# One decoder step on one core: cross attention of prompt and decode woven into one unrolled sequence

## The reference, cut to what matters

```python
def cross_attention(xn, mem_k, mem_v, w_xq, w_xo):
    q = (xn @ w_xq).reshape(B, T, 4, 256)
    s = jnp.einsum('bqhd,bkhd->bhqk', q, mem_k) * 256 ** -0.5
    p = jax.nn.softmax(s, axis=-1)
    o = jnp.einsum('bhqk,bkhd->bqhd', p, mem_v).reshape(B, T, 1024)
    return o @ w_xo
```

## Time and profile before

| what | us |
|---|---|
| median of 3 runs (2057.16 to 2065.2) | 2058.48 |
| the profiled execution, its own time | 2059.77 |
| its span in the trace | 2058.0 |
| PE busy in the span | 1851.6 (90%) |
| DVE, ACT, POOL busy | 956.0, 513.2, 107.2 |

### The profile page before, as it was taken

How to read it: one execution, slowest core, us unless ns; L and a number is a source line. 1 busy time by engine, 2 the same in 40 slices (tenths; PEclk the granted TensorE clock), 3 DMA queues, 4 the chain that set the end, 5 groups by cost and what they waited for, 6 DMA issues and landing times.

```text
span 2058.0 us, 32104 instructions
## 1 busy us (share of the span) xinstructions
PE 1851.6 (90%) x12971; PEld 1669.7 (81%) x12971; DVE 956.0 (46%) x1127; ACT 513.2 (25%) x847; POOL 107.2 (5%) x141
## 2 busy tenths in 40 slices
PE   6699998989988978898896969999999999999993
PEld 4599896656557977797745958999999999999992
DVE  2614777877764258423302256343324332333445
ACT  2411213666555111403331132111000110001122
POOL 0000001000220001001010010000000000000000
PEclk7899999999998989999997979999999999999995
DMA  6311115666784114111043112111111211121003
GB/s 163 110 59 61 61 61 162 201 176 193 244 307 173 61 52 133 60 61 62 0 164 123 41 41 105 41 49 53 41 41 47 55 41 41 45 57 36 33 26 156
DMA packets 136998, 187.18 MB, mean 91 GB/s; under 512 B 7752, under 2 KB 99082, under 8 KB 136390
## 3 DMA queue, kind: packets, MB, share of 16 engines
q1 hardware_dynamic: 122032, 120.74, 19.1%
q0 software_dynamic: 14192, 64.53, 8.9%
q10 hardware_dynamic: 686, 0.73, 0.1%
HBM read 165.65 MB, written 20.74 MB: 91 GB/s over the span
## 4 chain that ended last, share of the span: by engine, by line
PE 81%; DVE 6%; ACT 6%; DMA 3%; issue 3%; SPq 1%; DVEq 0%; POOLq 0%; ACTq 0%; POOL 0%
PE PS L1619 19%; PE PS L1620 19%; PE PS L1621 19%; PE PS L1609 7%; PE PS L1781 2%; PE PS L1803 2%; PE PS L1827 2%; DMA bias_rows<-BVEC 2%; PE PS L2106 2%; PE PS L2082 1%; PE PS L1696 1%; ACT KTS L681 1%; PE PS L2066 1%; PE PS L1634 1%; PE PS L1864 1%
## 5 line engine op out<-in xcount | busy, mean ns | idle before, releaser
L1619 PE MATMUL PS<-XH,WH 128*128 128x352 f32 x1992 | 643.1, 323 | 0.0
L1620 PE MATMUL PS<-XL,WH 128*128 128x352 f32 x1992 | 638.6, 321 | 0.0
L1621 PE MATMUL PS<-XH,WL 128*128 128x352 f32 x1992 | 638.3, 320 | 0.0
L1084 DVE CAST WH<-RAW 128x1024 fp32r<-128x1024 f32 x128 | 97.2, 760 | 719.9 <-PE PS L1621 695.0
L1620 PEld LDWEIGHTS PS<-XL,WH 128*128 128x128 f32 x1992 | 374.3, 188 | 0.0
L1619 PEld LDWEIGHTS PS<-XH,WH 128*128 128x128 f32 x1992 | 373.7, 188 | 0.0
L1621 PEld LDWEIGHTS PS<-XH,WL 128*128 128x128 f32 x1992 | 373.4, 187 | 0.0
L1086 DVE TENSOR_TENSOR WL<-RAW,WH 128x1024 fp32r<-128x1024 f32 x128 | 158.9, 1242 | 4.4
L1199 DVE SCALAR_TENSOR_TENSOR CY<-GP,DW,CY 128x1024 f32<-128x1024 f32 x124 | 158.5, 1278 | 1.0 <-DVE CY L1202 1.0
L1619 PE MATMUL PS<-HH,WH 128*128 128x352 f32 x462 | 149.0, 323 | 0.0
L1620 PE MATMUL PS<-HL,WH 128*128 128x352 f32 x462 | 148.1, 321 | 0.0
(11 more groups left out here) (322 smaller groups left out, 2321.8 us busy)
## 6 DMA issues: line engine op xcount, KB each, us to landing
PG<-in_cache_k SPq DMA_DIRECT2D x128, 256.0 KB, 3.0
PG<-in_cache_v SPq DMA_DIRECT2D x64, 256.0 KB, 4.1
PG<-in_cache_v POOLq DMA_DIRECT2D x64, 256.0 KB, 4.4
RAW<-in_w_gate SPq DMA_DIRECT2D x22, 512.0 KB, 3.9
RAW<-in_w_up SPq DMA_DIRECT2D x22, 512.0 KB, 5.1
RAW<-in_w_in SPq DMA_DIRECT2D x20, 512.0 KB, 4.6
h_spill<-H POOLq DMA_DIRECT2D x2, 4224.0 KB, 13.9
H<-h_spill POOLq DMA_DIRECT2D x2, 4224.0 KB, 13.7
```

The costliest lines, as they stand in the source:

```text
L1084: dve.tensor_copy(WH[v % 2][:, :, :], raw).then_inc(hi_done, 1)
L1619: pe.matmul(out, WH[u][:, k, :], xh[:, k, cols], start=(k == 0), stop=False)
L1620: pe.matmul(out, WH[u][:, k, :], xl[:, k, cols], start=False, stop=False)
L1621: mm = pe.matmul(out, WL[u][:, k, :], xh[:, k, cols], start=False, stop=(k == kt - 1))
```

## The change

- Prompt and decode run in one unrolled sequence of nine steps (q from 0 to 8). In steps 0 to 3, the keys of two decode sequences are turned and scored among the prompt's matmuls (`CROSS_K`); in step 4 comes the decode softmax; in steps 5, 6 and 7, the decode values of three, three and two sequences (`CROSS_V`).
- The turns of the keys have one PSUM bank in place of two. CKT has four buffers, one for each head, and the decode scores of a sequence are issued at once, with the head as the inner loop.
- The prompt's scores have one pair of banks in place of two, and read the queries straight from Y. Q2S and its copies are gone.
- CKV has four buffers. The first two lie in scratch space of the norm, and their loads are issued once the norm's sums are done, during the query projection; the next two as before, when the last `xq` tile is done.
- OX is copied and turned in step 8, ahead of the last block of prompt values.

The diff, cut; the removed lines are those of the kernel above. Left out too are the bodies of DVE functions that only change their place.

```diff
+        CKV = [at(f"CKV{i}", [P, 2, D], F32, (R2B + 16384, R2B + 24576, R1, R1 + 8192)[i]) for i in range(4)]
+        XP = [at(f"XP{i}", [P, NH, NMEM], F32, R1 + 16384 + 4096 * i) for i in range(2)]
+        XPT = [at(f"XPT{i}", [P, 8, P], F32, R1 + 24576 + 4096 * i) for i in range(2)]
+        CKT = [at(f"CKT{i}", [P, 2, NMEM], F32, R1 + 32768 + 2048 * i) for i in range(NH)]
+        XS = at("XS", [P, NMEM], F32, R1 + 40960)
+        OX = at("OX", [P, NMEM], F32, R1 + 41984)
+        YZ = at("YZ", [P, KT, DB * (TS + DS)], F32, R1 + 43008)
...
+        CROSS_K, CROSS_V = {q: (2 * q, 2 * q + 1) for q in range(4)}, {5: (0, 1, 2), 6: (3, 4, 5), 7: (6, 7)}
...
+            def memory_in(n):
+                pool.dma_start(CKV[n % 4][:, :, :], ck[n] if n < DB else cv[n - DB]).then_inc(ck_in[n % 4], 16)
+            pool.wait_ge(n_x["summed"], KT)
+            for n in range(2):
+                memory_in(n)
+            pool.wait_ge(tile_done, TILE0["xo"] + AHEAD)
+            for n in range(2, 4):
+                memory_in(n)
...
+            for n in range(4, 2 * DB):
+                if n - 4 < DB:
+                    pool.wait_ge(ck_turned, 4 * (n - 4) + 4)
                 else:
+                    pool.wait_ge(cv_used, n - 4 - DB + 1)
+                memory_in(n)
...
+            def memory_taken(b, h):
+                act.wait_ge(ck_turned, NH * b + h + 1)
+                if b:
+                    act.wait_ge(cs_done, b)
+                copy(CKT[h][:, :, :].rearrange("p a t -> p (a t)"), PS[:, 2, :]).then_inc(ck_taken, 1)
+            def cross_exp(q, h):
+                act.activation(XP[q % 2][:, h, :], PSF[:, NMEM * h:NMEM * (h + 1)], ACT.Exp,
+                               bias=XNM[q % 2][:, h:h + 1], scale=XSCALE, accum_out=XSUM[q % 2][:, h:h + 1])\
+                    .then_inc(x_p, 1)
+            for q in range(QT + 1):
+                b = CROSS_K.get(q)
+                if q:
+                    act.wait_ge(x_pt, q)
+                    if q >= 3:
+                        act.wait_ge(x_pv, q - 2)
+                    copy(XPT[(q - 1) % 2][:, :, :].rearrange("p (a k) t -> p a (k t)", a=2), PS[:, 4:6, :]).then_inc(x_ptok, 1)
+                if b:
+                    for h in range(NH):
+                        memory_taken(b[0], h)
+                if q < QT:
                     act.wait_ge(x_negmax, q + 1)
+                    if q >= 2:
+                        act.wait_ge(x_pt, q - 1)
                     for h in range(NH):
+                        cross_exp(q, h)
+                        if b:
+                            memory_taken(b[1], h)
+                if q == 4:
+                    act.wait_ge(xsm_v, 2)
+                    act.activation(XS[:, :], PS[:, 3, 0:NMEM], ACT.Exp, bias=XNMS, scale=XSCALE, accum_out=XSUMS)\
+                        .then_inc(xsm_a, 1)
...
+            for q in range(QT + 1):
+                if q < QT:
+                    cross_max(q)
+                if q == 4:
+                    decode_max_cross()
+                if q < QT:
+                    cross_weights(q)
+                if q == 4:
+                    decode_weights_cross()
+                if q == QT:
+                    dve.wait_ge(cv_used, DB)
+                    dve.tensor_copy(OX[:, :], PS[:, 3, 0:NMEM]).then_inc(xsm_v, 1)
+                    dve.wait_ge(xsm_p, 2)
+                    for a in range(2):
+                        dve.tensor_copy(Y[:, a:KT:2, TP:T], PS[:, 2, P * a:P * a + P].rearrange("p (h t) -> p h t", h=NH))\
+                            .then_inc(xsm_v, 1)
+                if q:
+                    cross_out(q - 1)
+                if q == 4:
+                    decode_turned_cross()
...
+            def cross_scores(q, h):
+                if h == 0:
+                    pe.wait_ge(x_p, NH * q)
+                for k in range(2):
+                    x = pe.matmul(PSF[:, NMEM * h:NMEM * h + NMEM], Y[:, 2 * h + k, P * q:P * q + P],
+                                  KMT[:, 2 * h + k, :], start=(k == 0), stop=(k == 1))
+                if h == NH - 1:
+                    x.then_inc(xs_done, 1)
+            def cross_turn(q):
                 pe.wait_ge(x_pn, q + 1)
                 pe.wait_ge(x_ptok, q)
                 for h in range(NH):
                     for k in range(2):
                         n = 2 * h + k
+                        x = turn(PS[:, 4 + n // 4, P * (n % 4):P * (n % 4) + P], XP[q % 2][:, h, P * k:P * k + P])
                 x.then_inc(x_pt, 1)
+            def cross_values(q, n):
+                if n == 0:
+                    pe.wait_ge(x_ptok, q + 1)
+                    pe.wait_ge(x_out, q)
+                for d in range(2 * n, 2 * n + 2):
                     for k in range(2):
                         x = pe.matmul(PS[:, 6 + d // 4, P * (d % 4):P * (d % 4) + P], VM[:, k, P * d:P * d + P],
+                                      XPT[q % 2][:, 2 * (d // 2) + k, :], start=(k == 0), stop=(k == 1))
+                if n == 3:
+                    x.then_inc(x_pv, 1)
+            def memory_turn(b, h):
+                if h == 0:
+                    pe.wait_ge(ck_in[b % 4], 16 * (b // 4) + 16)
+                pe.wait_ge(ck_taken, NH * b + h)
                 for d in range(2):
                     for a in range(2):
+                        c = 2 * h + d
+                        x = turn(PS[:, 2, NMEM * d + P * a:NMEM * d + P * a + P], CKV[b % 4][:, a, P * c:P * c + P])
+                x.then_inc(ck_turned, 1)
+            def memory_scores(b):
+                pe.wait_ge(ones_ok, 11)
+                pe.wait_ge(ck_taken, NH * b + NH)
+                for d in range(2):
+                    for h in range(NH):
+                        x = pe.matmul(PS[32 * h:32 * h + 32, 3, 0:NMEM], YZ[:, 2 * h + d, TS * b:TS * b + TS],
+                                      CKT[h][:, d, :], start=(b == 0 and d == 0), stop=(b == DB - 1 and d == 1))
+                x.then_inc(cs_done, 1)
...
+            def memory_values(b):
+                n = DB + b
+                pe.wait_ge(ck_in[n % 4], 16 * (n // 4) + 16)
+                if b == 0:
+                    pe.wait_ge(xsm_v, 6)
+                for a in range(2):
+                    for h in range(NH):
+                        x = pe.matmul(PS[32 * h:32 * h + 32, 3, 0:NMEM], PTZ[:, a, h, TS * b:TS * b + TS],
+                                      CKV[n % 4][:, a, NMEM * h:NMEM * h + NMEM],
                                       start=(b == 0 and a == 0), stop=(b == DB - 1 and a == 1))
                 x.then_inc(cv_used, 1)
+            pe.wait_ge(memkv_taken, 4)
+            pe.wait_ge(psum_free, TILE0["xo"] + AHEAD)
+            for q in range(QT + 1):
+                keys, vals = CROSS_K.get(q), CROSS_V.get(q, ())
+                if q:
+                    cross_turn(q - 1)
+                for h in range(NH):
+                    if keys:
+                        memory_turn(keys[0], h)
+                    if q < QT:
+                        cross_scores(q, h)
+                    if h == 0 and q - 1 in CROSS_K:
+                        memory_scores(CROSS_K[q - 1][1])
+                for b in vals:
+                    memory_values(b)
+                if q == QT:
+                    pe.wait_ge(xsm_v, 7)
+                    for a in range(2):
+                        x = turn(PS[:, 2, P * a:P * a + P], OX[:, P * a:P * a + P])
+                    x.then_inc(xsm_p, 1)
+                for n in range(4):
+                    if keys:
+                        memory_turn(keys[1], n)
+                    if n == 0 and keys:
+                        memory_scores(keys[0])
+                    if q:
+                        cross_values(q - 1, n)
+                if q == 4:
+                    pe.wait_ge(xsm_v, 4)
+                    for a in range(2):
+                        x = turn(PS[:, 2, P * a:P * a + P], XS[:, P * a:P * a + P])
+                    x.then_inc(xsm_p, 1)
```

More of the change, by code:

```diff
@@ L204, in hymba_step @@
         KMTOK = at("KMTOK", [P, 2, D], F32, R1 + 24576)
[L206 to L216 removed]
+        CKV = [at(f"CKV{i}", [P, 2, D], F32, (R2B + 16384, R2B + 24576, R1, R1 + 8192)[i]) for i in range(4)]
[5 more added lines that the diff above has]
+        YZ = at("YZ", [P, KT, DB * (TS + DS)], F32, R1 + 43008)
+        PTZ = at("PTZ", [P, 2, NH, DB * (TS + DS)], F32, R1 + 52224)
         HST = [at(f"HST{i}", [P, KT, P], F32, R1 + 4096 * i) for i in range(2)]
@@ L414, in hymba_step @@
         x_out = sem("x_out")
-        ck_in = [sem(f"ck_in{i}") for i in range(2)]
+        ck_in = [sem(f"ck_in{i}") for i in range(4)]
         ck_turned = sem("ck_turned")
@@ L1000, in _ @@
             late_norm(n_x, NM, "x_pre")
-            act.wait_ge(psum_free, TILE0["xo"] + AHEAD)
+            act.wait_ge(mem_v_out, 16)
             act.wait_ge(tile_done, TILE0["xo"] + AHEAD)
-            act.wait_ge(mem_v_out, 16)
-            def stage_query(q):
```

(37 more changed lines are left out.)

133 lines of the change are left out of this document (24 added, 109 removed).

## The result

| | before | changed |
|---|---|---|
| median, us (runs beside each other) | 2060.7 (4 runs) | 2010.1 (4 runs, 2006.3 to 2011.7) |
| profiled execution, span | 2059.77, 2058.0 | 2010.85, 2009.3 |
| stage: last query write to first matmul of `xo` | 943.92 to 1109.65: 165.7 | 942.69 to 1060.23: 117.5 |

The ratio is 0.9748 (95% interval 0.973 to 0.9767): 2.5% faster. The forecast was 2011.5, with 2004 to 2028. The stage is 48.2 us shorter and the span 48.7, so the gain is the stage's: it starts 1.2 us earlier, and what lies behind it takes 0.7 us longer.

What follows compares the result with a forecast made beforehand. PE's in-order list, its work and idle time, was taken to bound the stage. Steps summed to 116.3 us, 49.5 less; a second clock fall left 47.2 saved from 2059.77, 2012.6, median 2011.5, range 2004 to 2028.

Steps and rivals of the forecast that it cites:

- step 4: Last carried-over decode scores, a prompt block and the decode softmax: 11.1 us, with PE idle 1.8 before the XS turns.
- step 8: OX turns, last prompt values and output copies before `xo`: 9.8 us, of which 3.8 idle at the end.
- low rate: Rival: column groups take 1.96 us a sequence for scores and values, bound by weight issue; saved 32, 2026; chance 0.12.
- no overlap: Rival: decode scores still take 3.92 us a sequence in the new order; saved about 17, 2041; chance 0.05.
- second low spell: Second half of step 0: the granted clock falls once more amid short turns and waits, costing about 2.3 us.
- step 0: First key turns and prompt scores, with no values to put between: 8.2 and 7.3 us for its halves, 15.5 together.
- step 1: First of three like steps weaving key turns, prompt scores, decode scores and values: 15.9 us each, before any low spell.
- steps 5 to 7: Prompt blocks with three, three and two sequences of decode values at 1.0 us each: 32.1 us.
- first low spell: Start of step 0: PE spends 4.8 us at granted clock 0.50 after idling, losing 2.4 us.
- The rival in which steps 0 to 3 stay at half clock: Turns do not count as busy, so PE's work doubles there; saved about 25, 2033; chance 0.06.
- from the side of what goes: Cross-check for the whole stage: 63 us of work and waits removed, 14 of new idle time, difference 49.
- The slower case: Rival: the woven sequence never regains full clock, taking 208 us in place of 116; 43 slower, 2101; chance 0.03.

Runs made afterwards that it cites:

- the other edits: Changed kernel with three key turns ahead of the last query write and carried-over decode scores ahead of the first head's prompt scores: stage 111.0 us, median 2004.9.
- one head at a time: Changed kernel with each head's decode scores issued by themselves, other PE work between heads: stage 136.2 us, median 2030.5.
- the profiled run with early turns: Changed kernel with three key turns before the last query write and carried-over decode scores ahead of the first head's prompt scores: stage 111.0 us, median 2004.9.
- the one with the filler too: Changed kernel with early key turns, reordered decode scores and 32 useless matmuls between key turns of step 0's second half: stage 108.8 us, median 2004.1.

## Why the prediction was right

- **Column groups.** 1.0 us for 16 instructions was forecast from half of the low-clock 1.96; the trace has 1.00 for scores and 0.91 for values, at a granted clock of 1.00. Taking them apart again costs 18.7 us. The rivals "low rate" and "no overlap" fall. The Trainium skill ("TensorEngine Tiling (Array Packing)", Overview: Theoretical Speedup) gives up to 4 times for dimensions of 32 or less; here it is 3.9 times (3.92 to 1.0). Against 16 instructions at the plain 0.216 it is 3.5 times; the rest is what the lone head cost above that, 0.98 against 0.865.
- **Step by step.** Forecast and trace, with the second low spell added to step 1: step 0, 15.5 and 16.0; step 1, 18.2 and 17.4; steps 2 and 3, 15.9 and 15.6 each; step 4, 11.1 and 11.4; steps 5 to 7, 32.1 and 31.6; step 8, 9.8 and 9.9. Sum 118.6 and 117.5. Part of the closeness of step 0 is luck: PE starts 0.36 behind the query write, which was not counted, and the first low spell lasted longer, but a key turn with its head's scores takes 1.35 and not 1.445. The idle of 0.78 behind the first head is there to the digit, and so are the ones near 1.8 before XS and 3.8 before `xo`. The forecast 0.2 ahead of the second turn is not there; the last exponentials cost 0.38, not 0.28; the idle before the OX turns is 0.78, not 0.95; the values were 0.09 cheaper each.
- **The clock.** It fell twice, at the places named. The second spell was put at 2.3 us; filling the gaps gave back 2.0 in the changed kernel and 2.2 with the other edits. For the first, PE needed until about 948.8, 5.8 us after its start, where I took 4.8. The rival in which steps 0 to 3 stay at half clock falls: the clock was 1.00 from 976.12 to 1007.32, steps 2 and 3.
- **Loads.** No idle time of PE is put down to a load. That this hung on the four buffers, for steps 5 and 6, and not for the keys, was not in the forecast, which spoke of cover in general; the run with two buffers shows it.
- **Where the forecast was right in sum for partly compensating reasons.** The account "from the side of what goes" put 23 on the scores, 21 on the values and 19 on the rest. The runs give 14 to 19 for the groups, 10 to 14 for buffers and loads, depending on what stands beside them, and 20 for weaving, because weaving is also what takes loads and CKT copies out of PE's way and keeps the clock up under the values. The sum, 48, is the same; the split by cause needed the experiments.
- **Slips in the working that decided nothing.** The rival without overlap was priced at 30 us (17 saved in place of 47), where eight sequences at 3.92 in place of 1.0 make 23; one head at a time measured 18.7. The slower case was said to need some 110 us of low clock out of 116. By its own figures, all 116 at low clock add 92 us, so some 62 of them use up the 49.5 gained; those would last some 110, which is to be held against the 166 of the stage before. And the clock was said to fall in 826 to 828 "where PE made only turns": in the 6 us before that PE made only turns too, and the clock was 1.00 (last section).

## What to carry to other kernels

When an engine with an in-order list stalls in several small ways, walk the new order step by step with durations from the old trace, and for each wait ask what stands before it in every queue: here that gave the stage to 1 us in 118. The four-way split of the array paid here only with all four heads' operands there together, so it needed four copies of the operand's buffer, and then loads that keep up (17.6 us with four load buffers, 14.3 with two). And where a step must wait, put work there, real work first: real turns ahead of the query write, with the reordered scores, shortened the stage by 6.6 us, useless instructions in step 0 by 2.0 to 2.2.

## What the runs showed of the hardware that was not expected

**Useless matmuls made the kernel's stage shorter**, by 2.0 us alone and 2.2 with the other edits, by keeping the granted clock at 1.00. In the medians (2010.1 and 2008.7, 2004.9 and 2004.1) this doesn't stand out.

**Turns alone can hold the clock.** The Trainium skill ("TensorE: Matmul & The Clock Gate", Part 4: PE-mode transpose) says that transposes don't count as busy time in the way matmuls do. With three turns in the idle time before the query write, 0.77 of 2.00 us busy, the clock stayed at 1.00, and it fell when that time held nothing; so here turns did help, though in step 0 four turns with 0.7 to 1.1 us between them were not enough. The kernel before shows both too. From 819.9 PE makes only turns, eight at a time with 1.2 us between them, and the clock stays at 1.00 up to 826; then it falls:

```profile
822.00:824.00 2.00, 1.06 (x8) 0.85 (x8) 0.00 (x0) 0.76 (x2) 0.00 (x0) 1.00 0.67 195
824.00:826.00 2.00, 1.06 (x8) 0.86 (x8) 0.00 (x0) 0.75 (x2) 0.75 (x1) 1.00 1.00 346
```

What tells the cases apart was not tried.

**The same instructions ahead of the stage take a different time from one execution to the next.** The last query write ended at 938.8 us in the profiled run with early turns and at 948.6 in the one with the filler too, though the two kernels differ in nothing but that filler, which comes later. The window of the mixer from 330 to 520 us, in the first of the two and in the second:

```profile
330.00:520.00 190.00, 172.78 (x1948) 112.08 (x1948) 145.19 (x247) 122.31 (x279) 8.65 (x16) 0.99 0.67 202
```

```profile
330.00:520.00 190.00, 174.06 (x1885) 113.33 (x1887) 139.87 (x242) 120.34 (x272) 7.54 (x14) 0.96 0.66 197
```

The granted clock is 0.99 in the one and 0.96 in the other, and the second gets through fewer instructions in the same time (1885 of PE against 1948). That is why differences of under 10 us were read from the stage and not from the medians. What decides how often the clock falls in the mixer is open.
